# Local attention units two slots apart, Fourier steps behind them, the query's rotation swap two slots earlier

## The chip, the cores and the metric

The kernel runs on one core of a Trainium2 chip. The metric is the device time of one execution in microseconds (us); the time of before is the median of three runs. In the rows, PE is TensorE's matmul stream and PEld its weight loads, DVE is VectorE, ACT is ScalarE, POOL is GpSimd and SP is SyncE, which here only issues DMA transfers.

## The reference, cut to what matters

One sequence of 256 tokens of width 2048 passes a first block (gated delta rule and convolution mixer, cross attention to a memory, squared-ReLU MLP) and then a second block. The change lies in the second block's mixer:

```
cq, ckv, kr, qn, kn, vn, f = split_columns(h @ w_in)         # and the same of the context: ckv_c, kr_c, kn_c, vn_c
q_m, k_m, v_m = mla_qkv(cq, ckv, kr, ...)                    # rmsnorm, up projection, rotation of 64 features a head
o_mla = blocked_attention(q_m, [k_m, k_mc], [v_m, v_mc])     # 8 heads
o_na  = neighborhood_attention(qn, kn, vn, kn_c, vn_c, rpb)  # 4 heads, window plus context: softmax over 512 keys
o_fn  = fourier_mix(f, w_fnet)                               # 4 groups of 128 channels
x = x + gt1 * (concat([o_mla, o_na, o_fn]) @ w_out)
```

`axial_rope` rotates pairs of the query's and the key's 64 rotary features: `x * cos + swapped(x) * sin`. All values are float32.

## The kernel before, in words

All weights come as one stream of 906 slots of 512 KB, in the order of the phases of `phases()`. For each slot SP loads a raw tile (8 buffers), ACT writes its upper part `whi` (L922), DVE the remainder `wlo` (L1481, 4 buffers of each), and PE runs 24 matmuls on it (L465). ACT may write the upper part of slot s only when PE has finished slot s - 4, so ACT and DVE work about three slots ahead of PE. Two PSUM banks, 0 and 1, take turns as the target of a block of output columns. ACT (L934, L942) empties them in its own program order, in the iteration that lies three slots behind the block's last slot; PE waits with `block_free` until the block before the last has been emptied.

Work that is no weight matmul is put into the stream by hand. Each engine's program calls, behind each slot, a function of the slot number (`extra`, `tail`; `local` for the region of the change), and nothing else orders it: each engine runs its own list strictly in order, and semaphores hold it back. Slots are counted here from the phase `fn`: fn 0 to 7, ckv_x 8 to 15, cq 16 to 23, kr_x 24 and 25, kn_c 26 to 29, v_c 30 to 33, kn_x 34 to 37, v_x 38 to 41, qr 42 and 43, qn 44 to 47; wout2 begins at 48. `LOCAL_AT` holds these numbers.

Local attention has 8 units (4 heads by 2 halves of the queries). Step u, behind the slot `NA_PE[u]` on PE, multiplies the scores of unit u (L712), transposes the probabilities of unit u - 1 (L724), and at odd u from 3 on multiplies a head's values (L744). DVE takes the scaled and biased scores and their maximum (`attention_max`, L1893 to L1898) in its iteration s = `NA_PE[u]` + 3 and divides by the sum (`attention_scale`, L1904 and L1905) in iteration `NA_PE[u]` + 4; ACT does the exponential (L1188) and the copies (L1198, L1207) in iteration `NA_PE[u]` + 4. In an iteration of DVE the maximum stands ahead of the scale.

The Fourier mixing has 6 steps, behind the slots `FN_PE`. Step n multiplies the stage of group n (L835), the second stage of group n - 1 (L830) and the last of group n - 2 (L824); ACT copies each result (L1336, L1333, L1329) in iteration `FN_PE[n]` + 3.

Between them run the norms of the latent vectors: squares on ACT (L1311), their sum on DVE (L2051), a root (L1317, L2063), scaling (L2069), and the split of the result into the activation tile `act` (L1322 on ACT, L2075 on DVE). `act_in(n)` on PE waits for n such splits ahead of kn_c, kn_x and qr. `heads_upper(q)` and `heads_lower(q)` (L1375, L2080) split the outputs of local attention (q = 2) and of the Fourier mixing (q = 3) into `act` in the same way.

The rotation: PE swaps the features by a matmul with a permutation (L859 for the key, L863, four of them, for the query), and DVE's `rope` makes three operations of each (L2092 to L2094). PE waits ahead of the attention over the latents (`attention("mla")`: L715, L716, L724, L744) until all are done and until the last block of qn has been emptied (`phase_out`).

Of the kernel before, what the change touches and what calls it, by code (L numbers as in the profile page):

```python
# [26 lines left out]
MLA_H, NOPE, ROPE, LAT = 8, 128, 64, 512  # L27
# [72 lines left out]
PH, N_SLOTS = phases()  # L100
# [26 lines left out]
def build(nc, x_t, mem_t, ctx_t, stream, mods, pvec, eye, cmix, catt, na_bias, na_mask, out_t):  # L127
    es = ExitStack()
    with es:
        def sb(name, shape, dt=F32, stack=None):  # L130
            return (stack or es).enter_context(nc.sbuf_tensor(name, shape, dt))
# [9 lines left out]
        act = sb("act", [P, 2, DC, T], F32R)  # L141
# [279 lines left out]
        LOCAL_AT = {}  # L421
        for name in ("fn", "ckv_x", "cq", "kr_x", "kn_c", "v_c", "kn_x", "v_x", "qr", "qn"):
            LOCAL_AT[name] = PH[name].slot0 - PH["fn"].slot0
        NA_PE = (3, 4, 6, 7, 9, 10, 12, 13, 15, 16)
        FN_PE = (17, 19, 21, 23, 25, 26)
        LAT_BANK = (7, 5, 6)

        def attention_units(kind):
# [7 lines left out]
        def _(pe):  # L436
# [93 lines left out]
            def act_in(n):  # L530
                c.at(act_ready, n)
                c.end(act_ready, n)
# [305 lines left out]
            def local(name):  # L838

                def f(i, j):  # L840
                    s = LOCAL_AT[name] + j
                    if s in NA_PE:
                        if s == NA_PE[0]:
                            phase_out(PH["naq"])
                        attention_step("na", NA_PE.index(s))
                    if s in FN_PE:
                        if s == FN_PE[0]:
                            pe.wait_ge(late_in, 16)
                        fourier_step(FN_PE.index(s))
                    if s == LOCAL_AT["cq"] + 6:  # L850
                        latent_sum(1)
                    if s == LOCAL_AT["kn_c"] + 1:
                        latent_spread(1)
                    if s == LOCAL_AT["kn_c"] + 3:
                        latent_sum(2)
                    if s == LOCAL_AT["kn_x"] + 1:
                        latent_spread(2)
                    if s == LOCAL_AT["kn_x"] + 2:
                        pe.matmul(bank[3][:, 0:T], cc(CA, "swap"), kr[:, 0, :], start=True, stop=True).then_inc(rope_pe, 1)  # L859
                    if s == LOCAL_AT["qn"] + 3:  # L860
                        phase_out(PH["qr"])
                        for n in range(MLA_H // 2):
                            pe.matmul(bank[4 + n][:, 0:T], cc(CA, "swap"), qR[:, n, :], start=True, stop=True).then_inc(rope_pe, 1)  # L863
                return f
# [16 lines left out]
                phase(PH[name], act, extra=local(name))  # L881
            act_in(1)
            phase(PH["kn_c"], act, extra=local("kn_c"))
            phase(PH["v_c"], act)
            act_in(1 + 2)
            phase(PH["kn_x"], act, 4, extra=local("kn_x"))
            phase(PH["v_x"], act, 4)
            act_in(1)
            phase(PH["qr"], act)
            phase(PH["qn"], act, extra=local("qn"))  # L890
            phase_out(PH["qn"])
# [20 lines left out]
        def _(sc):  # L912
# [427 lines left out]
            def local(name, ahead=False):  # L1340

                def f(i, j):
                    if j >= PH[name].S or (j < PRE) != ahead:
                        return
                    s = LOCAL_AT[name] + j
                    if s - 4 in NA_PE:
                        attention_step("na", NA_PE.index(s - 4))
                    if s - 3 in FN_PE:
                        fourier_step(FN_PE.index(s - 3))
                    if s == LOCAL_AT["cq"] + 4:  # L1350
                        sc.wait_ge(block_free, FREE + PH["ckv_x"].block0 + 2)
                        latent_square(1, ckv[:, 0, :, :])
                    if s == LOCAL_AT["kn_c"] + 1:
                        sc.wait_ge(block_free, FREE + PH["cq"].block0 + 2)
                        sc.wait_ge(lat_part, 2)
                        latent_square(2, cq[:, :, :])
                    if s == LOCAL_AT["kn_c"] + 0:
                        latent_sqrt(1)
                    if s == LOCAL_AT["v_c"] + 0:
                        heads_upper(2)  # L1360
                    if s == LOCAL_AT["v_c"] + 1:
                        heads_upper(3)
                    if s == LOCAL_AT["v_c"] + 2:
                        latent_upper(1, LC, ckv[:, 0, :, :])
                    if s == LOCAL_AT["v_c"] + 3:
                        latent_sqrt(2)
                    if s == LOCAL_AT["v_x"] + 2:
                        sc.wait_ge(slot_used, SPL_N + PH["v_c"].slot0 + PH["v_c"].slots)
                        latent_upper(2, 0, cq[:, :, :])
                return f  # L1370
# [59 lines left out]
        def _(ve):  # L1430
# [147 lines left out]
            def phase(name, evac, extra=None, tail=None):  # L1578
                ph = PH[name]
                over(ph, slot, evac(ph), extra, tail)  # L1580
# [484 lines left out]
            def latent_norm(n, src, gain):  # L2065

                ve.wait_ge(lat_spread, n + 1)
                for k in range(LC):
                    ins = ve.scalar_tensor_tensor(src[:, k, :], src[:, k, :], par(gain, k), bank[LAT_BANK[n]][:, T:2 * T], ALU.mult, ALU.mult)  # L2069
                ins.then_inc(lat_normed, 1)  # L2070
# [6 lines left out]
            def heads_lower(q):  # L2077

                c.at(norm_hi, q - 1)
                ve.tensor_tensor(act[:, 1, 4 * q:4 * q + 4, :], tmp[:, 4 * q:4 * q + 4, :],  # L2080
                                 act[:, 0, 4 * q:4 * q + 4, :].bitcast(F32), ALU.subtract).then_inc(act_ready, 1)
                if q == 3:
                    c.end(norm_hi, 2)
                    c.end(head_hi, NA_H + FN_G)

            def rope(n):

                x_ = kr[:, 0, :] if n == 0 else qR[:, n - 1, :]
                c.at(rope_pe, n + 1)
                if n:  # L2090
                    c.at(rope_dve, n)
                ve.tensor_tensor(stat[:, 0, 0:T], x_, cc(CA, "cos"), ALU.mult)  # L2092
                chain(ve.tensor_tensor(stat[:, 1, 0:T], bank[3 + n][:, 0:T], cc(CA, "sin"), ALU.mult))
                ve.tensor_tensor(x_, stat[:, 0, 0:T], stat[:, 1, 0:T], ALU.add).then_inc(rope_dve, 1)  # L2094
# [21 lines left out]
            def local(name, ahead=False):  # L2116

                def f(i, j):
                    if j >= PH[name].S or (j < PRE) != ahead:
                        return  # L2120
                    s = LOCAL_AT[name] + j
                    if s - 3 in NA_PE and s - 3 <= NA_PE[7]:
                        attention_max("na", NA_PE.index(s - 3))
                    if s - 4 in NA_PE and s - 4 <= NA_PE[7]:
                        attention_scale("na", NA_PE.index(s - 4))
                        if s - 4 == NA_PE[7]:
                            attention_end("na")
                    if s == LOCAL_AT["cq"] + 5:
                        latent_part(1)
                    if s == LOCAL_AT["kr_x"] + 1:  # L2130
                        latent_var(1)
                    if s == LOCAL_AT["kn_c"] + 1:
                        latent_root(1)
                    if s == LOCAL_AT["kn_c"] + 2:
                        latent_part(2)
                    if s == LOCAL_AT["v_c"] + 0:
                        heads_lower(2)
                    if s == LOCAL_AT["v_c"] + 1:
                        latent_norm(1, ckv[:, 0, :, :], "g_kv")
                    if s == LOCAL_AT["v_c"] + 2:  # L2140
                        heads_lower(3)
                        latent_lower(1, LC, ckv[:, 0, :, :])
                    if s == LOCAL_AT["v_c"] + 3:
                        latent_var(2)
                    if s == LOCAL_AT["kn_x"] + 0:
                        latent_root(2)
                    if s == LOCAL_AT["v_x"] + 0:
                        rope(0)
                    if s == LOCAL_AT["v_x"] + 1:
                        latent_norm(2, cq[:, :, :], "g_q")  # L2150
                    if s == LOCAL_AT["v_x"] + 2:
                        latent_lower(2, 0, cq[:, :, :])
                return f
# [18 lines left out]
            for name, then in (("kn_c", "v_c"), ("v_c", "kn_x"), ("kn_x", "v_x")):  # L2172
                phase(name, nothing, local(name), into(then))
            phase("v_x", nothing, local("v_x"))
            phase("qr", nothing)
            phase("qn", nothing)
            for n in range(1, 1 + MLA_H // 2):
                rope(n)
            attention("mla")
            residual("wout2", 32)  # L2180
            norm(h, gs(GAIN_F), shift=48)
# [151 lines left out]
```

## Time and profile before

| what | value |
|---|---|
| median of 3 runs | 2984.42 us (2977.87 to 2985.08) |
| profiled execution, first to last instruction | 2987.6 us |
| TensorE granted clock, mean | 0.980 |
| PE busy | 2856.1 us (96%) |
| DVE busy | 2091.8 us (70%) |
| ACT busy | 1349.8 us (45%) |
| DMA | 591.59 MB, mean 198 GB/s |

The span is the only time that the profile gives of the profiled execution; it is 3.2 us above the median. A granted clock of 1.00 is 2.4 GHz, one of 0.50 is 1.2 GHz. In the chain of waits a row is a start, a length and what ran; where a row of PE follows rows of DVE or ACT, PE had nothing to do in between.

### The profile page before, as it was taken

To read this page: it belongs to the slowest core of one execution; us is meant where nothing else is said; L and a number is where in the kernel's file an instruction comes from. 1 tells how busy PE (TensorE), PEld (TensorE's weight loads), DVE (VectorE), ACT (ScalarE), POOL (GpSimd) and SP (SyncE) were. 2 spreads that over 40 slices of the span, in tenths; PEclk is the share of its full clock that TensorE was granted. 3 is DMA by queue.
4 is the path that set the end of the run, shared out by engine and by line. 5 is a ranking of instruction groups with operands and counts; after the bars stand their busy time and mean duration, and the time that the engine had idled before them with its cause. 6 is when DMAs were issued, how large, how long until landed. Compare 5 with 4: busy or idle time off the path is not lost.

```text
span 2987.6 us, 55330 instructions
## 1 busy us (share of the span) xinstructions
PE 2856.1 (96%) x23894; PEld 2799.2 (94%) x23894; DVE 2091.8 (70%) x2910; ACT 1349.8 (45%) x1702; POOL 5.1 (0%) x13
## 2 busy tenths in 40 slices
PE   7998888999999999999999999999998999999998
PEld 7998888999998999999999999888698999999998
DVE  6988654698886978777777867545457665765665
ACT  4445423344443554444545545445345444454443
POOL 0000000000000000000000000000000000000000
PEclk9999899999999999999999999999999999999999
DMA  5555201567773787777777775434064555556553
GB/s 204 188 170 163 77 1 60 191 240 269 270 280 127 250 301 285 273 277 293 274 284 290 261 245 187 151 110 156 29 190 148 198 198 192 192 191 202 184 198 120
DMA packets 160452, 591.59 MB, mean 198 GB/s; under 512 B 17840, under 2 KB 17840, under 8 KB 159696
## 3 DMA queue, kind: packets, MB, share of 16 engines
q1 hardware_dynamic: 159264, 579.93, 55.9%
q0 software_dynamic: 944, 8.12, 0.7%
q8 instruction: 188, 3.08, 0.4%
q14 instruction: 56, 0.46, 0.0%
HBM read 585.88 MB, written 2.10 MB: 197 GB/s over the span
## 4 chain that ended last, share of the span: by engine, by line
PE 86%; DVE 9%; ACT 3%; issue 1%; DMA 1%; SPq 0%; DVEq 0%; ACTq 0%
PE bank L465 76%; DVE wlo L1481 3%; PE bank L744 1%; DVE ev L1500 1%; DVE modacc L1714 1%; PE bank L492 1%; PE bank L639 1%; PE bank L482 1%; PE bank L637 1%; ACT whi L922 1%; PE bank L631 1%; PE bank L496 1%; PE bank L716 1%; DVE modacc L1467 1%; PE bank L724 1%
## 5 line engine op out<-in xcount | busy, mean ns | idle before, releaser
L465 PE MATMUL bank<-act,whi 128*128 128x256 f32 x10144 | 1765.6, 280 | 43.5 <-DVE wlo L1481 26.7
L465 PEld LDWEIGHTS bank<-act,whi 128*128 128x128 f32 x10144 | 1549.4, 190 | 49.8 <-DVE wlo L1481 23.4
L1481 DVE TENSOR_TENSOR wlo<-raw,whi 128x1024 fp32r<-128x1024 f32 x906 | 1096.8, 1221 | 483.9 <-ACT whi L922 482.4
L465 PE MATMUL bank<-act,wlo 128*128 128x256 f32 x5072 | 1416.0, 279 | 0.0
L922 ACT ACTIVATE whi<-raw 128x1024 fp32r<-128x1024 f32 x906 | 942.9, 1056 | 798.1 <-PE bank L465 797.1
L465 PEld LDWEIGHTS bank<-act,wlo 128*128 128x128 f32 x5072 | 963.5, 190 | 0.0
L465 PE MATMUL bank<-hid,whi 128*128 128x256 f32 x3456 | 590.1, 277 | 1.5 <-DVE wlo L1481 1.5
L465 PEld LDWEIGHTS bank<-hid,whi 128*128 128x128 f32 x3456 | 521.0, 188 | 1.9 <-DVE wlo L1481 1.3
L465 PE MATMUL bank<-hid,wlo 128*128 128x256 f32 x1728 | 478.5, 277 | 0.0
L1467 DVE SCALAR_TENSOR_TENSOR modacc<-modraw,small,modacc 128x512 f32<-128x512 f32 x480 | 348.3, 746 | 16.5 <-DMA modraw<-mods 11.9
L465 PEld LDWEIGHTS bank<-hid,wlo 128*128 128x128 f32 x1728 | 324.5, 188 | 0.0
L465 PE MATMUL bank<-whi,act 128*128 128x256 f32 x896 | 156.7, 279 | 0.5 <-ACT kN L934 0.5
L465 PEld LDWEIGHTS bank<-whi,act 128*128 128x128 f32 x896 | 136.1, 188 | 0.7 <-ACT kN L934 0.7
L465 PE MATMUL bank<-wlo,act 128*128 128x256 f32 x448 | 124.8, 279 | 0.0
L1561 DVE SCALAR_TENSOR_TENSOR ev<-bank,pv,ev 128x255 f32<-128x255 f32 x176 | 76.9, 478 | 62.9 <-ACT ev L987 61.4
L1714 DVE SCALAR_TENSOR_TENSOR modacc<-modraw,modacc 128x256 f32<-128x256 f32 x232 | 98.4, 477 | 0.1
L465 PEld LDWEIGHTS bank<-wlo,act 128*128 128x128 f32 x448 | 84.2, 188 | 0.0
L987 ACT ACTIVATE ev<-bank,pv 128x256 f32<-128x256 f32 x88 | 44.9, 560 | 70.4 <-PE bank L465 70.4
L1000 ACT ACTIVATE ev<-h 128x512 f32<-128x512 f32 x32 | 20.2, 632 | 115.8 <-DVE h L1536 69.4
L1550 DVE TENSOR_TENSOR hid<-ev,hid 128x512 fp32r<-128x512 f32 x32 | 22.1, 692 | 67.5 <-ACT hid L976 67.5
L992 ACT ACTIVATE ev<-ev 128x256 f32<-128x256 f32 x44 | 18.4, 418 | 80.1 <-DVE ev L1561 80.1
L1125 ACT ACTIVATE tmp<-bank 128x512 f32<-128x512 f32 x28 | 16.7, 597 | 73.5 <-PE bank L631 73.5
(315 smaller groups left out, 1586.4 us busy)
## 6 DMA issues: line engine op xcount, KB each, us to landing
raw<-stream SPq DMA_DIRECT2D x906, 512.0 KB, 4.5
modraw<-mods SPq DMA_DIRECT2D x192, 512.0 KB, 4.4
h<-x_t SPq DMA_DIRECT2D x4, 512.0 KB, 5.8
memV<-mem_t POOLq DMA_DIRECT2D x1, 2048.0 KB, 9.1
tmp<-ctx_t POOLq DMA_DIRECT2D x1, 2048.0 KB, 9.8
out_t<-tmp SPq DMA_DIRECT2D x4, 512.0 KB, 2.6
cz<-catt POOLq DMA_DIRECT2D x1, 1216.0 KB, 12.8
bias<-na_bias POOLq DMA_DIRECT2D x1, 1024.0 KB, 5.0
```

The source lines that it names most:

```text
L465: mm = pe.matmul(b[:, hf * T:(hf + 1) * T], lhs, rhs, start=(kc == 0 and hf == 0 and n == 0), stop=(kc == ph.chunks - 1 and n == 2), skip_ ...
L482: mm = pe.matmul(bank[2][:, 4 * w + n:4 * w + n + 1], modacc[:, w, n * P:(n + 1) * P], ones[:, 0:1], start=True, stop=True, skip_group_che ...
L492: return pe.matmul(out, src[:, tok], ones[:, 0:1], start=start, stop=stop, skip_group_check=True)
L496: return pe.matmul(out, small[:, col + n:col + n + 1].to_broadcast([P, P]), ident[:, :], start=start, stop=True, skip_group_check=True)
L631: mm = pe.matmul(bk(hg, 0)[:, n, :], MT[hg][:, n, :], X[hg][:, n, :], start=True, stop=True)
L637: pe.matmul(bk(hg, 2)[:, n, :], XT[hg][:, n, :], Y[hg][:, n, :], start=True, stop=True)
L922: sc.activation(whi[:, at % SPL_N, :], raw[:, at % RAW_N, :], ACT.Copy).then_inc(hi_done, 1)
L987: ins = sc.activation(ev[:, 0, hf * T:(hf + 1) * T], b2(b)[:, hf, :], ACT.Identity, scale=par("ff_conv", n * 6 + (6 * first + 3 * hf + 1)) ...
L1467: ins = ve.scalar_tensor_tensor(acc, wt, col, acc, ALU.mult, ALU.add)
L1481: ve.tensor_tensor(wlo[:, at % SPL_N, :], raw[:, at % RAW_N, :], whi[:, at % SPL_N, :].bitcast(F32), ALU.subtract).then_inc(split_done, 1)
L1561: ins = ve.scalar_tensor_tensor(o, b2(b)[:, hf, so], par("ff_conv", n * 6 + (6 * first + 3 * hf + j)), o, ALU.mult, ALU.add)
L1714: ins = ve.scalar_tensor_tensor(acc, x_, w, acc, ALU.mult, ALU.add)
```

## The change

The local attention's steps come behind every second slot from 3 to 21 and its Fourier steps behind slots 22 to 32. The split of the Fourier outputs moves from v_c to kn_x on ACT and DVE, and the counts in PE's `act_in` with it; PE's phase v_c gets the `local` function, as Fourier steps now fall into it. The swap of the query's rotary features is issued behind slot 45 in place of slot 47, and DVE's four rotations stand behind its own slot 47, ahead of slots 48 to 50, where before they stood behind slot 50.

```diff
-        NA_PE = (3, 4, 6, 7, 9, 10, 12, 13, 15, 16)
-        FN_PE = (17, 19, 21, 23, 25, 26)
+        NA_PE = (3, 5, 7, 9, 11, 13, 15, 17, 19, 21)
+        FN_PE = (22, 24, 26, 28, 30, 32)
...
-                    if s == LOCAL_AT["qn"] + 3:
+                    if s == LOCAL_AT["qn"] + 1:
                         phase_out(PH["qr"])
                         for n in range(MLA_H // 2):
                             pe.matmul(bank[4 + n][:, 0:T], cc(CA, "swap"), qR[:, n, :], start=True, stop=True).then_inc(rope_pe, 1)
...
-            phase(PH["v_c"], act)
-            act_in(1 + 2)
+            phase(PH["v_c"], act, extra=local("v_c"))
+            act_in(1 + 1)
             phase(PH["kn_x"], act, 4, extra=local("kn_x"))
             phase(PH["v_x"], act, 4)
-            act_in(1)
+            act_in(1 + 1)
...
-                    if s == LOCAL_AT["v_c"] + 1:
+                    if s == LOCAL_AT["kn_x"] + 2:
                         heads_upper(3)
...
+                    if s == LOCAL_AT["kn_x"] + 3:
+                        heads_lower(3)
                     if s == LOCAL_AT["v_c"] + 2:
-                        heads_lower(3)
                         latent_lower(1, LC, ckv[:, 0, :, :])
...
+            def query_ropes(i, j):
+                if j == PH["qn"].S - 1:
+                    for n in range(1, 1 + MLA_H // 2):
+                        rope(n)
             phase("qr", nothing)
-            phase("qn", nothing)
-            for n in range(1, 1 + MLA_H // 2):
-                rope(n)
+            phase("qn", nothing, query_ropes)
             attention("mla")
```

## Rows read from the trace of the kernel before

**Rows 1.** The page, part 1: busy us (share of the span) xinstructions.

```profile
PE 2856.1 (96%) x23894; PEld 2799.2 (94%) x23894; DVE 2091.8 (70%) x2910; ACT 1349.8 (45%) x1702; POOL 5.1 (0%) x13
```

**Rows 2.** Chain of waits, local attention: start us, length us, engine, tile, line, count.

```profile
1910.33 0.87 PE bank L712 x2
...
1912.01 0.70 DVE small L1896
...
1913.53 0.66 PE bank L724 x4
1914.19 5.46 PE bank L465 x48
...
1937.19 0.44 PE bank L724 x4
...
1957.14 0.87 PE bank L712 x2
...
1964.39 5.68 PE bank L465 x48
...
1973.24 1.73 PE bank L744 x8
```

**Rows 3.** Waits, 1905 to 1978 us: who waited for whom, total, times, longest.

```profile
PE bank L724 <- DVE stat L1905: 9.4, 4, 2.4
```

**Rows 4.** Windows: from:to us, length, busy us (count) per engine, clock, DMA share, GB/s.

```profile
1910.30:1914.20 3.90, 1.55 (x9) 0.72 (x8) 2.98 (x8) 1.99 (x5) 0.00 (x0) 1.00 0.41 134
...
1957.20:1964.40 7.20, 4.85 (x16) 3.34 (x15) 3.85 (x9) 1.87 (x3) 0.00 (x0) 0.76 0.46 146
...
2012.00:2020.00 8.00, 5.33 (x31) 5.23 (x31) 2.95 (x3) 2.74 (x5) 0.00 (x0) 0.79 0.37 124
...
2086.30:2102.00 15.70, 15.70 (x25) 5.16 (x26) 4.54 (x13) 3.31 (x8) 0.00 (x0) 0.57 0.00 1
```

**Rows 5.** Chain of waits, Fourier steps and the start of kn_c.

```profile
2003.56 0.86 PE bank L835 x4
...
2010.32 1.74 PE bank L830 x8
...
2012.36 1.06 ACT act L1322
...
2013.44 1.23 DVE act L2075
...
2014.72 4.62 PE bank L465 x24
```

**Rows 6.** Timeline of ACT and DVE: start, length, engine, line, operation, operands [idle before].

```profile
2007.43 1.05 ACT L1311 ACTIVATE tmp<-cq 128x1024 f32<-128x1024 f32 x1
...
2008.38 1.04 ACT L922 ACTIVATE whi<-raw 128x1024 fp32r<-128x1024 f32 x1
...
2010.60 1.91 DVE L2051 TENSOR_REDUCE tmp<-tmp 128x256 f32<-128x1024 f32 x1
...
2049.44 0.43 DVE L2092 TENSOR_TENSOR stat<-kr,cz 128x256 f32<-128x256 f32 x1 [3.62 <-PE bank L859]
```

**Rows 7.** Chain of waits, end of qn and start of the latent attention.

```profile
2080.41 0.45 PE bank L863 x2
...
2086.22 1.10 PE bank L715 x2
...
2101.91 0.59 PE bank L724 x4
```

**Rows 8.** Chain of waits, start of the first block's cross attention.

```profile
890.12 0.60 ACT tmp L934
...
892.80 0.43 DVE small L1896
...
896.14 0.44 PE bank L724 x2
```

**Rows 9.** Windows, the same cross attention.

```profile
890.00:895.00 5.00, 3.81 (x17) 2.96 (x16) 0.84 (x3) 2.03 (x3) 0.00 (x0) 1.00 0.93 308
```

## The prediction

> **What bounds the kernel now.** I read the page first: PE is busy for 96% of the span [rows 1], so a slot costs what its 24 matmuls cost, 2.73 us (half of the 5.46 us of 48) [rows 2], and a change that leaves the matmuls alone can only win where PE stands still or runs at the lower clock. Then I read the chain of waits from slot 3 of `fn` to the end of the latent attention, for the places where a row of DVE or ACT stands between rows of PE. There are four kinds: four waits in local attention, one ahead of kn_c, one of half a microsecond in v_x, and one ahead of the latent attention. The waits view names their partner [rows 3], the windows show the granted clock beside them [rows 4].
>
> **Local attention.** The reader should see the order on DVE: scores of unit 1 at 1910.33, then DVE's maximum of them at 1912.01, and only then the scale (L1905) of unit 0, for which PE's transposes at 1913.53 wait [rows 2, 3]. That is program order: with steps at slots 3 and 4, DVE's iteration 7 holds the maximum of unit 1 and behind it the scale of unit 0, so PE waits for a result that stands behind the scores it has just made. PE is idle from 1910.33 + 0.87 = 1911.20 to 1913.53, 2.33 us, four times in this stretch [rows 3]; the fifth adjacent pair (15, 16) has no unit left for the maximum, and its values at 1973.24 follow without a wait [rows 2]. The first step takes 1914.19 - 1910.33 = 3.86 us. Its work is 0.87 + 0.44 = 1.31 us, so 2.55 us are lost. The last of the four takes 1964.39 - 1957.14 = 7.25 us for 1.31 + 1.73 = 3.04 us of work: 4.2 us lost [rows 2], 2.33 of it the wait and 1.9 a clock of 0.76 in that stretch; the first ran at 1.00 [rows 4]. The two between are like the last. Sum: 2.55 + 3 x 4.2 = 15.2 us, of which 9.3 are waits and 5.9 clock.
>
> With steps two slots apart, maximum and scale of neighbouring units never share an iteration. From the end of a unit's scores (t = 0) the chain of maximum, exponential and scale takes 2.33 us plus an exponential and one split of a slot on DVE (1.2 us, the size of L2075 [rows 5]), some 4.3 us; the transposes come no sooner than 2 x 2.73 = 5.5 us later. So 1.2 us is spare in every step, and I cost the new spacing at nothing. If that cover were gone on all eight units for a microsecond, it would cost 8 us. Bounds of this part: 9.3 us (waits only) to 15.6.
>
> **Fourier steps.** The same matmuls are issued, so their work on PE (up to 0.43 + 1.74 + 0.86 us a step [rows 5]; the 0.43 is half of L835's four matmuls) only moves. Their ACT copies now share the iterations of kn_c and v_c with a block to empty behind every slot. Counting ACT behind a slot with a full step, from the slot's end: the step ends on PE at 3.0, ACT's copy of its last stage at 3.65 (0.60 long, the size of L934 [rows 8]), the block's emptying, also 0.60, at 4.25. PE needs that bank at the end of the next slot, 3.0 + 2.73 = 5.75. Spare 1.5 us, cost nothing. `heads_upper(3)` and `heads_lower(3)` go to iterations 36 and 37, 1.06 and 1.23 us. DVE waits 3.62 us there for the key's swap [rows 6], which hides the 1.23; uncovered, they would cost 2.3 us.
>
> **The start of kn_c gets worse.** Before, PE's Fourier step 4 stands behind slot 25 and ends at 2012.06. ACT's split L1322, held behind that step's copy, starts at 2012.36, DVE's L2075 follows, and PE resumes at 2014.72: a wait of 2.66 us, and the slot behind it takes 4.62 in place of 2.73, 1.9 us of clock (0.79 in that stretch [rows 4]) [rows 5]. DVE's sum of squares L2051, 1.91 us from 2010.60, lay beside this and was over before L2075 could begin [rows 6]. Afterwards step 1 (L830, L835, 1.74 + 0.86 = 2.6 us) stands behind slot 24. From the end of slot 24: slot 25 ends at 2.6 + 2.73 = 5.3. ACT copies L835's result at 2.6, starts the squares L1311 at 3.1 and the upper part of slot 28 0.95 later, at 4.05 (the distance of L1311 and L922 [rows 6]), done at 5.1. DVE takes slot 28 until 6.3, then the sum of squares until 8.2, then L2075 until 9.4, because `latent_part(2)` stands ahead of `latent_lower(0)` in iteration 28. PE waits from 5.3 to 9.5, 4.2 us, where it waited 2.66: 1.5 us lost. Bounds: with L2051 out of the way ACT's 1.06 and DVE's 1.23 alone would leave 2.4 us, a gain of 0.2; a longer fall of the clock here, as long as that ahead of the latent attention (below), would cost some 5 us more. I take -1.5, since every term of it is a row.
>
> **The query's rotation.** Before, PE's swap starts at the end of slot 47, 2080.41, DVE's four rotations follow, and attention starts at 2086.22: 5.81 us [rows 7]. Afterwards the four swaps (8 matmuls, as L830 x8, 1.74 us [rows 5]) stand ahead of slot 46. The first is there 0.45 us after slot 45, and the rotations are done at most 5.81 - 0.45 = 5.36 us later, at 5.8; slot 47 ends at 1.74 + 5.46 = 7.2. So 1.4 us is spare. What is late next is the emptying of the last block of qn: by the same hand-over at the cross attention, ACT's 0.60 us copy and 0.05 us around it [rows 8], PE starts 0.65 us after slot 47. Cost 1.74 + 0.65 = 2.4 in place of 5.81: 3.4 us won. On DVE the remainders of slots 48 to 50 now stand behind the rotations, 3 x 1.23 = 3.7 us of work that ends 5.8 + 3.7 - 7.2 = 2.3 us after slot 47; the first scores, two pairs of the size of L712 (0.87 [rows 2]) behind the 0.65, end at 2.4, so next to nothing waits, and what is missing there would cost its own length. SP's loads into those raw buffers go out a few us later, for slots that are not wanted until the attention is over. Bounds of this part: 0, were DVE late by all its cover and more, to 4.1 (no hand-over).
>
> The clock goes with it. From 2086.30 to 2102.00 it was 0.57 on average with PE busy all the time [rows 4], behind a standstill of 4.1 us. At full clock the same work takes 15.7 x 0.57 = 8.9 us, plus a wait behind the first scores, 0.5 by my estimate (0 to the 2.33 of [rows 3]): 9.4 in place of 15.7, 6.2 us won if the clock holds. The nearest row is the cross attention: a standstill of the same 0.65 us, then another of 3.3 us from 892.80 to 896.14, with a clock of 1.00 [rows 8, 9]. Bounds 0 to 6.7; I take 6.2.
>
> The Trainium skill, page TensorE: Matmul & The Clock Gate, section Why this matters for your kernels, lets the clock fall only over an idle gap longer than any of the four local waits. The trace does not agree: the last of the four 2.33 us waits has a clock of 0.76 beside it [rows 4], and the two before it are like it, while the 3.3 us at the cross attention have 1.00 [rows 9].
>
> **Sum.** 15.2 - 1.5 + 3.4 + 6.2 = 23.3 us. The profiled execution would go from 2987.6 to 2964.3; its span is all it has, and it lies 3.2 us above the median, so for the median 2984.42 - 23.3 = 2961.1. The small wait ahead of slot 39 in v_x stays: none of its terms is touched.
>
> **Rivals.**
> - *The clock falls at the start of the latent attention all the same.* For it: fp32 scores there kept 0.57 for 15.7 us, and one standstill of 0.65 and one of 0.5 us remain. Against it: [rows 9]. Gain 23.3 - 6.2 = 17.1: 2967.3.
> - *The falls of the clock are not the waits' doing* and lie elsewhere afterwards. For it: the first local wait had 1.00, the cross attention too. Then only standstill is won, 9.3 + 3.4 - 1.5 = 11.2: 2973.2. This is also what the page's rule would give for the local part.
> - *A new wait in the crowded iterations of ACT and DVE* (26 to 37, or the two-slot spacing), 1 us in each of some eight slots, because the 1.2 to 1.5 us of cover is missing: gain 15: 2969.
> - *Slower: the longer wait ahead of kn_c takes the clock down for the phases behind it.* A standstill of 4.1 us ahead of the latent attention went with 14 us of low clock; that of 4.2 us ahead of kn_c is as long. Each slot at half clock costs 2.73 us more. From 9 slots on (24.6 us) the change is a loss; over all 22 slots to the end of qn it is 60 us: 3021. Against it: behind the 2.66 us wait in the same place dense slots followed and the mean over the next 8 us was back at 0.79 [rows 4].
> - *It doesn't do what it says*: the transposes would still wait for DVE, were the wait one for the maximum's length and not its place. DVE's order in [rows 2] speaks against it: the maximum fills the wait; gain 23.3 - 15.2 = 8.1: 2976.3.
>
> **How the numbers follow.** Forecast 0.58, range of its own 2956 to 2966; clock low in the latent attention 0.17; clock elsewhere 0.08; new waits 0.10; slower 0.03; no effect in local attention 0.04. Low end: all upper bounds, 15.6 + 0.2 + 4.1 + 6.7 = 26.6 us, give 2957.8, less 4 us of spread (the three runs of before lie 7.2 us apart): 2954. High end: 2974, which takes in the rival without clock. A measurement of this kernel can tell 0.3%, 9.0 us, from no change. Faster by more than that is all above 2975.5 left out: 0.58 + 0.17 + 0.10 and most of the 0.08, some of it lost to spread, 0.90; within it 0.07; slower 0.03.
>
> **What would show it.** In local attention the transposes L724 have no idle time before them, odd steps take 3.0 us, and the clock is 1.00 from 1910 to 1975. Ahead of kn_c the chain shows L2051 between a split of a slot and L2075, and a wait of about 4.2 us. Ahead of L715 stand L934 and 0.65 us, not L2094, and L716's fourth pair ends about 9.4 us after the first begins. In kn_c and v_c no slot waits for L934. The prediction is wrong if a wait for L934 appears there, if DVE's L1896 of the first latent unit waits behind L1481, or if the clock shows falls of the old size with no standstill ahead of them.

## The result and the profile after

| | before | after |
|---|---|---|
| median, 20 runs each | 2985.38 us (2977.87 to 3017.3) | 2962.38 us (2956.14 to 2996.09) |
| ratio, with its 95% interval | | 0.9929 (0.9904 to 0.9954) |
| profiled span | 2987.6 us | 2963.5 us |
| mean granted clock | 0.980 | 0.985 |

The forecast for the median was 2961.1 us, for the profiled span 2964.3. Some runs of both kernels (4 of 20 before, 5 of 20 after) are some 28 us longer than the rest, and so are some runs of every kernel below but e8, which widens the intervals and shifts the medians. The parts are therefore read from the traces, in the stretch from the first local score (L712) to the first matmul of wout2: 1906.72 to 2149.50 = 242.8 us before, 1904.47 to 2125.31 = 220.8 us after, 21.9 us less. The other 2.2 us of the spans (24.1 in all) lie ahead of the stretch, where nothing was changed. Over the ten profiles of this document L712 first starts between 1898.43 us (e7) and 1909.17 (e4), so 2.2 us there says nothing. Behind the stretch both kernels take 838.1 to 838.2 us.

The chain of waits of after in local attention (start, length, what ran), the rows that answer to [rows 2]:

```profile
1910.80 0.86 PE bank L712 x2
1911.66 0.44 PE bank L724 x4
1912.10 5.46 PE bank L465 x48
...
1924.31 0.86 PE bank L712 x2
1925.17 0.44 PE bank L724 x4
1925.60 1.73 PE bank L744 x8
```

Scores, transposes and values follow each other with no row of DVE between them; a step is 1.30 or 3.03 us, as its work is. The row of [rows 3] is gone, and the window over the whole part (length, busy us of PE, PEld, DVE, ACT, POOL, clock, DMA share, GB/s) has PE busy throughout at 1.00, where [rows 4] had 0.76:

```profile
1910.00:1975.00 65.00, 65.00 (x503) 60.35 (x501) 37.70 (x61) 31.91 (x49) 0.00 (x0) 1.00 0.47 152
```

The start of kn_c in the chain of after, which answers to [rows 5]:

```profile
1982.41 0.88 PE bank L835 x4
...
1983.80 1.05 ACT tmp L1311
1984.85 0.96 ACT whi L922
...
1985.83 1.23 DVE wlo L1481
1987.06 1.82 DVE tmp L2051
1988.88 1.14 DVE act L2075
...
1990.07 5.49 PE bank L465 x24
1995.56 0.84 PE bank L824 x2
```

The reader should see that the chain runs through ACT's squares and split and then through three operations of DVE, of which only the last, L2075, is what PE needs. PE's slot 25 ends at 1983.29 + 2.73 = 1986.02, so it stands still for 4.05 us; the slot behind takes 5.49 us, twice its usual time, and the next small step 0.84 in place of 0.43. The window over these two has half the clock:

```profile
1990.07:1996.40 6.33, 6.33 (x27) 6.15 (x28) 1.08 (x1) 0.00 (x0) 0.00 (x0) 0.51 0.25 83
```

The start of the latent attention, which answers to [rows 7]:

```profile
2059.84 1.73 PE bank L863 x8
2061.56 5.67 PE bank L465 x48
...
2067.25 0.61 ACT tmp L934
...
2067.90 1.12 PE bank L715 x2
...
2072.58 0.66 PE bank L724 x4
...
2077.66 0.66 PE bank L724 x4
```

No rotation stands in this chain any more. L934, the last block of qn, does, and attention begins 0.67 us behind slot 47; its fourth pair of scores ends at 2077.65, 9.75 us after the first begins, against 15.7 before. Inside it PE waits once, 0.4 us, for the first L724. The window over it has full clock:

```profile
2067.00:2078.00 11.00, 9.91 (x29) 3.51 (x29) 6.61 (x15) 5.19 (x10) 0.00 (x0) 1.00 0.43 144
```

### The profile page after: what moved, and what is told of

It is laid out like the page before. It is cut to its first block, busy times and chain, and to the rows that moved or that the text cites. A ratio compares the mean times of both kernels' runs of the same rounds, so it can differ in the third digit from the quotient of the medians.

```text
span 2963.5 us, 55330 instructions
## 1 busy us (share of the span) xinstructions
PE 2845.2 (96%) x23894; PEld 2795.2 (94%) x23894; DVE 2091.9 (71%) x2910; ACT 1349.7 (46%) x1702; POOL 5.1 (0%) x13
## 4 chain that ended last, share of the span: by engine, by line
PE 86%; DVE 9%; ACT 2%; issue 1%; DMA 1%; SPq 0%; DVEq 0%; ACTq 0%
PE bank L465 76%; DVE wlo L1481 3%; PE bank L744 1%; DVE ev L1500 1%; DVE modacc L1714 1%; PE bank L492 1%; PE bank L639 1%; PE bank L482 1%; ACT whi L922 1%; PE bank L637 1%; PE bank L631 1%; PE bank L496 1%; DVE modacc L1467 1%; PE bank L716 1%; PE bank L724 0%
```

## The experiments

All were timed in rounds beside the kernel before. "Stretch" is the one above: 242.8 us before, 220.8 after. The ratio is taken from all runs and is not the quotient of the two medians (e5: 0.9997, its medians 0.9977).

| kernel | median us (before beside it) | ratio, interval | stretch us |
|---|---|---|---|
| e1, local part only | 2970.73 (2984.21) | 0.9954, 0.9918 to 0.9991 | 228.2 |
| e2, rotations only | 2974.50 (2984.21) | 0.9966, 0.9928 to 1.0004 | 232.5 |
| e3, sum of squares later | 2963.63 (2984.21) | 0.9924, 0.9885 to 0.9962 | 218.1 |
| e4, scale first | 2970.51 (2984.21) | 0.9955, 0.9921 to 0.9989 | 225.8 |
| e5, swap early, rotations late | 2975.52 (2982.41) | 0.9997, 0.9965 to 1.0030 | 231.9 |
| e6, Fourier step in the gap | 2955.57 (2982.41) | 0.9926, 0.9896 to 0.9956 | 213.7 |
| e7, hand-overs | 2964.23 (2982.41) | 0.9947, 0.9908 to 0.9986 | 218.8 |
| e8, e6 and e7 together | 2957.55 (2982.41) | 0.9905, 0.9877 to 0.9933 | 212.1 |

### e1: the local part alone

The changed kernel with three edits undone:

```diff
-                    if s == LOCAL_AT["qn"] + 1:
+                    if s == LOCAL_AT["qn"] + 3:
                         phase_out(PH["qr"])
...
-            phase("qn", nothing, query_ropes)
+            phase("qn", nothing)
+            for n in range(1, 1 + MLA_H // 2):
+                rope(n)
```

> The changed kernel with the query's swap and rotations put back to where they were (behind slot 47 on PE, behind slot 50 on DVE). Theory: the parts add up. From the two traces the local and Fourier part is worth 15.6 us of local waits and clock, less 2.8 us around the start of kn_c, so this kernel is 12.8 us faster than before, 2972.5; its trace shows the 5.8 us ahead of the latent attention and the clock near 0.57 behind them again. Rival (the falls of the clock are not the waits' doing and only move): the clock stays at 1.00 at the latent attention, and the gain is 19 us or, if falls turn up in local attention, about 7.

Measured: 13.5 us faster than before by the medians. The chain shows the standstill between the last rotation and L715 again, with the low clock behind it:

```profile
2067.69 0.44 DVE qR L2094
...
2068.26 2.01 PE bank L715 x2
```

```profile
2068.26:2078.50 10.24, 10.24 (x14) 3.18 (x14) 2.77 (x8) 2.04 (x5) 0.00 (x0) 0.50 0.00 0
```

So the clock did not stay at 1.00 there by itself: the rival is out. The low stretch is 10.2 us long here, against 13.7 in the profile of before.

### e2: the rotations alone

The kernel before, with the same three edits made.

> The kernel before with the swap and the rotations alone moved. Theory: 3.4 us of standstill and 5.9 us of clock are won, 9.3 us, 2976; the four local waits of 2.33 us and the 2.66 us ahead of kn_c stand as before, and the clock is 1.00 from the first scores of the latent attention on. Rival (the clock there falls whatever stands ahead of it): 3.4 us, 2982.

Measured: 9.7 us faster by the medians, though the interval just reaches 1, so the timings alone do not show a gain. The trace does. The four local waits are there as before, the standstill ahead of L715 is 0.67 us, and the clock behind it is 1.00:

```profile
PE bank L724 <- DVE stat L1905: 9.4, 4, 2.4
```

```profile
2079.00:2092.00 13.00, 11.92 (x41) 5.33 (x40) 7.69 (x18) 5.96 (x12) 0.00 (x0) 1.00 0.39 122
```

In the stretch e1 wins 14.6 us and e2 10.3, 3 us more together than the change. The standstills add up as they should; the clock's share does not. e2 has a clock of 1.00 behind its wait of 2.66 us ahead of kn_c, and the slot there takes 2.99 us where before's takes 4.62 (1.6 us); e1's low stretch in the latent attention is 3.4 us shorter than before's, 1.7 us at half clock. These two are 3.3 of the 3 us. In local attention e2 loses as much to the clock as before does, 68.25 us over the whole part in both, but the wait that has no fall behind it is the second of the four in e2 and the first in before.

### e3: DVE's sum of squares behind the split that PE waits for

```diff
-                    if s == LOCAL_AT["kn_c"] + 2:
+                    if s == LOCAL_AT["kn_c"] + 3:
                         latent_part(2)
```

> The changed kernel with DVE's sum of squares of the query latents (L2051) one iteration later, behind slot 29 in place of 28, so that it stands behind the split L2075 for which PE waits ahead of kn_c. Theory (the longer wait is DVE's program order): the wait goes from 4.05 to 2.4 us, and with it one of the two low stretches of the clock, together 3 us faster than the changed kernel, 24.5 us faster than before. Rival (ACT is what is late, by the Fourier copies and squares in iteration 27): the wait stays within 0.3 us of 4.05 and the time is that of the changed kernel.

```profile
1983.28 2.84 PE bank L465 x24
...
1986.14 1.07 ACT act L1322
...
1987.23 1.24 DVE act L2075
...
1988.51 4.60 PE bank L465 x24
```

Only the two halves of the split are left in the chain. The wait is 1988.51 - 1986.12 = 2.4 us, the slot behind it 4.60 us and not 5.49; the stretch is 2.8 us shorter than that of after, as expected. The median, 20.6 us below that of before where 24.5 were expected, does not resolve so little.

### e4: the old spacing, with the scale ahead of the maximum

```diff
-                    if s - 3 in NA_PE and s - 3 <= NA_PE[7]:
-                        attention_max("na", NA_PE.index(s - 3))
                     if s - 4 in NA_PE and s - 4 <= NA_PE[7]:
                         attention_scale("na", NA_PE.index(s - 4))
                         if s - 4 == NA_PE[7]:
                             attention_end("na")
+                    if s - 3 in NA_PE and s - 3 <= NA_PE[7]:
+                        attention_max("na", NA_PE.index(s - 3))
```

> The kernel before, steps one slot apart, with one thing changed: in DVE's iteration the scale of unit u - 1 stands ahead of the maximum of unit u. Theory (the local wait is DVE's order, not the distance): the scale no longer needs the new scores; counted from the end of slot s, DVE has the scale of unit s at about 4.3 us while PE ends the scores of the next at 0.87 + 2.73 + 0.87 = 4.5, so the four waits shrink from 2.33 to under 0.3 us and the time falls by 9 us of wait and up to 6 of clock, 2970 to 2976. Rival (one slot is too short for maximum, exponential and scale in any order): the waits stay above 1.5 us and the time within 5 us of before.

```profile
1912.78 0.86 PE bank L712 x2
...
1913.65 0.66 PE bank L724 x4
...
1923.80 0.86 PE bank L712 x2
1924.66 0.44 PE bank L724 x4
1925.10 1.73 PE bank L744 x8
```

```profile
1909.00:1975.00 66.00, 65.98 (x493) 60.24 (x492) 38.03 (x65) 34.59 (x55) 0.00 (x0) 1.00 0.41 134
```

All four waits are gone (the first leaves 0.02 us) with the units one slot apart, and 13.7 us of time with them, as much as e1 wins. Local attention takes 53.05 us in place of before's 68.25, with the same 13 slots in it: 15.2 us won. So the wait was the order of two calls in one iteration of DVE. The spacing of the change cures it by never putting the two into one iteration. Swapping them does the same, and leaves the Fourier steps and the wait ahead of kn_c as they were.

### e5: the swap early, the rotations late

The changed kernel with the DVE part of e1's edit only.

> The changed kernel with PE's swap behind slot 45 as in the change, but DVE's four rotations behind its slot 50, where they were before. Theory (the 3.4 us come from DVE starting behind slot 47 and not from the swap alone): DVE's slot 50 ends 1.06 + 1.23 us behind PE's slot 46, 0.4 us ahead of the end of slot 47, the rotations follow with 5.3 us, and attention starts about 4.9 us after slot 47 with the clock low behind it for 10 us or more: 4.2 + 6 us slower than the changed kernel, near 2971. Rival (the swap's place is what counts): attention starts 0.7 us after slot 47 and the time is that of the changed kernel.

```profile
2064.61 0.04 DVE wlo L1481
...
2065.75 0.42 DVE stat L2092
...
2070.51 0.44 DVE qR L2094
...
2071.08 2.04 PE bank L715 x2
```

Slot 47 ends at 2063.01 + 2.73 = 2065.7 and attention starts 5.3 us later (4.9 expected, as the last remainder and its hand-over to the rotations take 0.4 more); the stretch is 11.0 us longer than after's (10.2 expected), 4.7 of standstill and the rest mostly the clock. The interval of its ratio takes in 1, so by the timings alone e5 can't be told from before. PE's swap alone buys nothing (e1, with neither moved, has a stretch 3.7 us shorter than e5's); the place of DVE's rotations is what counts.

### e6: a Fourier step where PE waits

```diff
-        FN_PE = (22, 24, 26, 28, 30, 32)
+        FN_PE = (22, 23, 25, 27, 29, 31)
...                                        # ACT, into()
-                    if j < PRE:
-                        local(name, ahead=True)(0, j)
                     if then:
                         then(j)
+                    if j < PRE:
+                        local(name, ahead=True)(0, j)
```

and e3's edit.

> The changed kernel with Fourier steps behind slots 22, 23, 25, 27, 29, 31, so that the full step of 3.03 us stands behind slot 25, where PE waits; ACT's split of the context latent (L1322) ahead of that step's copies in iteration 28, and DVE's sum of squares one iteration later. Theory (PE waits 4.05 us there only because it has nothing in hand): the split takes 1.06 + 1.24 us and is done while PE runs the step; no wait and no fall of the clock ahead of kn_c, 4.05 + 2.8 to 3.2 us of clock, 7 us faster than the changed kernel, near 2954. Rival (ACT, with steps one slot apart at 22 and 23 and the root's table load between, is late with the copies, and PE waits at slots 23 to 25 in place of 26): less than 3 us won, waits of PE for L1333 or L1336 in the chain.

```profile
1986.85 0.43 PE bank L824 x2
1987.29 1.73 PE bank L830 x8
1989.01 0.86 PE bank L835 x4
1989.88 5.46 PE bank L465 x48
```

```profile
1975.00:2000.00 25.00, 25.00 (x182) 23.91 (x182) 9.49 (x10) 14.91 (x23) 0.00 (x0) 1.00 0.33 107
```

PE goes from the step straight into kn_c; the wait is not shortened but filled, and the clock stays up. The stretch is 7.1 us shorter than after's, 7 were expected.

### e7 and e8: the two hand-overs, and all together

e7 is the changed kernel with

```diff
-            phase_out(PH["qn"])
+            pe.wait_ge(block_free, FREE + PH["qn"].block0 + PH["qn"].nblocks - 1)
             c.at(rope_dve, 1 + MLA_H // 2)
-            attention("mla")
+            for u in range(len(attention_units("mla")) + 2):
+                if u == 3:
+                    phase_out(PH["qn"])
+                attention_step("mla", u)
...                                        # ACT, and the same on DVE for latent_lower(2, ...)
-                    if s == LOCAL_AT["v_x"] + 2:
+                    if s == LOCAL_AT["v_x"] + 3:
                         sc.wait_ge(slot_used, SPL_N + PH["v_c"].slot0 + PH["v_c"].slots)
                         latent_upper(2, 0, cq[:, :, :])
```

> The changed kernel with two hand-overs eased: attention over the latents starts when three of the four blocks of qn are emptied and waits for the last one ahead of its step 3; the split of the query's latent (L1322, L2075) stands in iteration 41 in place of 40, behind the emptying of kn_x's last block. Theory: 0.65 us ahead of L715 and 0.6 us ahead of slot 39 in v_x go, 1.3 us in all, below what the median can tell; the trace shows neither L934 in the chain. Rival (the next wait takes their place: DVE's rotations at the first, L2075 ahead of qr at the second): the chain shows them and under 0.3 us is won.

> The two before it together. Theory: 7 + 1.3 us, 8.3 us faster than the changed kernel, near 2953, 1.0% faster than before. Rival: with the last standstills gone nothing is left in the stretch but the waits behind the first and the last scores of the latent attention, and what was a wait elsewhere comes up in its place: under 5 us.

e8's chain, from the key's swap to the first scores of the latent attention:

```profile
2029.57 0.43 PE bank L859 x2
2030.01 24.94 PE bank L465 x216
2054.95 1.73 PE bank L863 x8
2056.68 5.65 PE bank L465 x48
2062.33 0.86 PE bank L715 x2
```

PE is the only engine in it. e7 shortens the stretch by 2.0 us against after (1.3 expected; 0.4 of the rest is the small step behind kn_c's first slot, 0.43 us in place of 0.84), e8 by 8.7 (8.3 expected), and the rivals' new waits did not come up. e6 and e8 have the shortest stretches of all. By their medians they are 26.8 and 24.9 us faster than before, the changed kernel 23.0 and e7 18.2; between these four the timings can't tell. In e8's stretch PE stands still only from the latent attention on; ahead of it the clock is 1.00 throughout:

```profile
1907.36:2062.33 154.97, 154.97 (x1219) 148.26 (x1219) 87.21 (x125) 85.91 (x123) 0.00 (x0) 1.00 0.44 143
```

## Why the prediction was right

**Local attention** (said: 15.2 us won). From the first score to the end of step 9 before took 1974.97 - 1906.72 = 68.25 us with 13 slots of 2.73, after 1971.08 - 1904.47 = 66.61 with 18: 32.8 and 17.5 us beside the slots, 15.3 won. The reason given, DVE's program order, is what e4 shows. The clock's share, 5.9 us, was won back together with the waits in e1, e4 and after.

**Fourier steps** (said: nothing). In the waits view of after no slot of kn_c, v_c or kn_x waits on an emptying of a bank that it did not wait on before; the 0.5 us ahead of slot 39 in v_x stayed, as said, until e7.

**The start of kn_c** (said: 1.5 us lost). The wait went from 2.66 to 4.05 us; 4.2 had been worked out, through the same operations in the same order. e3 confirms its cause. The mis-sized term is the clock, which the sum left as it was: behind the longer wait it stayed low over the whole slot and the step after it, 0.87 + 0.41 = 1.3 us more than before. The part costs 2.7 us, inside the bounds named.

**The query's rotation** (said: 3.4 us of standstill and 6.2 of clock). From the end of slot 47 to wout2 before took 69.09 us; after takes 58.08 and 1.73 of swaps, 9.3 won. The start came 1.73 + 0.67 = 2.4 us, as said; the first four pairs took 9.75 us and not 9.4. DVE's remainders of slots 48 to 50 were done 1.2 us before it got the first scores, so none of that cover was missing. e2 shows this part alone, e5 that it hangs on DVE.

15.3 - 2.7 + 9.3 = 21.9, the difference of the stretches. The forecast of 23.3 was 1.4 too high there, and 2.2 us ahead of the stretch made it up: so part of the agreement of the spans (2963.5 against 2964.3) is chance. Between 280 and 400 us, in a stage that the change doesn't touch, the windows have a mean clock of 0.84 before and 0.90 after, and of 0.84 to 0.90 in the other profiles.

**The rivals.** The clock of the latent attention stayed up. That the falls of the clock are not the waits' doing is answered by e1, e2 and e4: where the waits went the falls went (1.00 over 66 us in e4), where they stayed, most falls stayed. No new wait came up, and the lower clock behind kn_c lasted for one slot and a step, not for the phases behind it.

**What the prediction misread.** Its nearest row for a clock that holds was the cross attention, with a standstill of 0.65 us and "then another of 3.3 us from 892.80 to 896.14" [rows 8, 9]. The chain shows only the work that ended last, so a row of DVE between two of PE does not by itself mean, as the text ahead of the prediction has it, that PE had nothing to do. PE's own timeline, and the window behind it:

```profile
890.77 3.72 PE L709 MATMUL bank<-memK,tmp 128*128 128x256 f32 x16 [0.69 <-ACT tmp L934]
896.14 0.44 PE L724 MATMUL bank<-ident,stat 128*128 128x128 f32 x2 [1.65 <-DVE stat L1905]
```

```profile
895.00:900.00 5.00, 3.86 (x20) 3.31 (x20) 2.44 (x10) 2.36 (x8) 0.00 (x0) 1.00 0.10 40
```

PE made scores until 894.49 and stood still for 1.65 us, not 3.3. So that row shows a clock of 1.00 with standstills of 0.69 and 1.65 us, both shorter than the local waits. It did support a clock that holds behind 0.65 us, and after and e2 bore that out, but it says nothing on a gap of 3.3 us.

The page of the Trainium skill named in the prediction (TensorE: Matmul & The Clock Gate, Why this matters for your kernels) would have had the local waits do no harm; the traces of before and e2, with three low stretches behind four waits of 2.33 us, do not agree with it. The prediction's second ground against the page, the 3.3 us, falls away with the misreading.

## What to carry to other kernels

When an engine on the critical path waits for a result of another, look in the waited engine's program for what stands ahead of it in the same iteration: here the order of two calls (e4) won as much as the new spacing of ten steps, and one call moved by one iteration (e3) took back 2.8 us that the spacing had cost. A wait that can't be shortened can be filled, if the step that fills it has its inputs ready and the waited engines do the urgent work first (e6). Count with a standstill of the size seen here (2.33 us and more) also the low clock behind it, as a range of its own. And before a gap between two rows of the chain is called a standstill of PE, look at PE's own timeline: the chain leaves out what PE does beside it.

## What the runs showed of the hardware

- The low clock behind a standstill is no constant. Behind 2.33 us in local attention it came three times out of four, in before and in e2, but not behind the same three. Behind the wait ahead of kn_c it cost 1.9 us in before (2.66 us) and e3 (2.4 us), 1.6 in e4 (2.66 us) and at most 0.3 in e2 (2.66 us), and 2.7 to 3.2 us behind the 4.05 us of after, e1, e5 and e7. Ahead of the latent attention a standstill of 4.1 us had 10.2 us at half clock behind it in e1 and e4 and 13.7 in before, one of 5.3 us had 17.1 in e5, with PE busy. Standstills of 0.67 us there had 1.00 behind them in after, e2 and e6, and the 1.65 us in before's cross attention too.
- The same matmuls run at two rates that the granted clock does not show. In e3's profiled run the feed-forward phases from up_0 on are one unbroken row in the chain, as they are in after's, with the same matmuls and windows of 100 us at a clock of 0.99 to 1.00, and take 28 us more: 747.85 against 719.72 us, 118.0 ns a matmul against 113.6. The profiles of e5 and e7 have this long row too. Both rates also occur within one execution: the 768 matmuls of wout2 take 90.7 us (118.1 ns) in after and 87.3 us (113.7 ns) in e3, at a clock of 1.00 in both, so the profile with the slower feed-forward has the faster wout2. What sets the rate was not found. The row of after, then that of e3:

```profile
2228.87 719.72 PE bank L465 x6336
```

```profile
2221.87 747.85 PE bank L465 x6336
```

The windows over wout2, of after and of e3:

```profile
2125.31:2216.05 90.74, 90.72 (x768) 90.52 (x768) 49.44 (x53) 36.96 (x39) 0.00 (x0) 1.00 0.57 180
```

```profile
2122.54:2209.80 87.26, 87.26 (x768) 87.12 (x768) 49.41 (x53) 37.01 (x39) 0.00 (x0) 1.00 0.58 188
```
